# Stick-breaking attention on one core: sums of later key blocks with low parts on GpSimd, the last pair in a new order, and a weight panel's high part on GpSimd

## What is computed

```python
z = einsum('bqhd,bkhd->bhqk', q, k) * HD_B ** -0.5 + bias
u = where(mask, log_sigmoid(-z), 0.0)                # mask: key strictly before query
rev_excl = cumsum(u, axis=3, reverse=True) - u       # sum over later keys
A = where(mask, exp(log_sigmoid(z) + rev_excl), 0.0)
out = einsum('bhqk,bkhd->bqhd', A, v)
h = h + out @ w_out_b                                # output projection
```

## Time and profile before

| | us |
|---|---|
| median of 3 runs (1500.52 to 1502.69) | 1500.58 |
| the profiled execution | 1502.18 |
| its span, first to last instruction | 1500.4 |
| TensorE busy | 1476.8 |
| VectorE busy | 1181.6 |
| ScalarE busy | 827.7 |
| GpSimd busy | 333.6 |

### The profile page before, as it was taken

The page is one execution under the profiler, slowest core; times in us unless marked ns, Lnnn a source line. Parts: engine busy times, 40 slices in busy tenths (PEclk is TensorE's granted clock), DMA queues, the critical chain, the costliest instruction groups (busy, mean ns, idle before and its releaser), DMA issues.

```text
span 1500.4 us, 33609 instructions
## 1 busy us (share of the span) xinstructions
PE 1476.8 (98%) x12928; PEld 1397.7 (93%) x12928; DVE 1181.6 (79%) x2014; ACT 827.7 (55%) x1312; POOL 333.6 (22%) x330
## 2 busy tenths in 40 slices
PE   8999999999999999999999999999999999999998
PEld 8999999989999999999998888887699999999998
DVE  7866666667898988989834888888789989898753
ACT  6554444435664645546533777777756546364543
POOL 3000000002332232232142122112233332232221
PEclk9999999999999999999999999999999999999999
DMA  6233333223777877777425555543338777778621
GB/s 191 58 87 88 87 87 87 87 87 87 139 170 157 179 164 161 176 153 155 135 85 176 186 191 197 184 156 114 100 86 168 177 159 168 166 157 187 142 85 64
DMA packets 237716, 205.83 MB, mean 137 GB/s; under 512 B 8268, under 2 KB 224404, under 8 KB 237588
## 3 DMA queue, kind: packets, MB, share of 16 engines
q1 hardware_dynamic: 151346, 147.34, 31.6%
q0 software_dynamic: 68160, 47.20, 20.4%
q10 hardware_dynamic: 18082, 9.48, 2.3%
HBM read 192.19 MB, written 11.80 MB: 136 GB/s over the span
## 4 chain that ended last, share of the span: by engine, by line
PE 94%; DVE 2%; ACT 2%; issue 1%; DMA 0%; DVEq 0%; ACTq 0%
PE acc L2904 23%; PE acc L3227 18%; PE pL L3227 12%; PE pM L3227 9%; PE acc L3327 6%; PE pO L3227 3%; PE acc L3165 2%; PE pL L3025 1%; PE pL L3368 1%; PE pO L3401 1%; PE pM L3382 1%; PE acc L3444 1%; PE acc L3461 1%; PE pM L3094 1%; PE pM L3388 1%
## 5 line engine op out<-in xcount | busy, mean ns | idle before, releaser
L658 POOL TENSOR_TENSOR wlo<-wraw,whi 128x512 fp32r<-128x512 f32 x40 | 56.2, 1435 | 449.3 <-ACT whi L795 449.3
L2904 PE MATMUL acc<-xa_hi,whi 128*128 128x288 f32 x544 | 125.0, 311 | 0.2 <-DVE hT L2355 0.2
L881 ACT ACTIVATE hi<-wraw 128x1024 fp32r<-128x1024 f32 x60 | 63.7, 1061 | 104.2 <-DVE wraw L2025 104.2
L864 ACT ACTIVATE hi<-wraw 128x1024 fp32r<-128x1024 f32 x60 | 63.7, 1061 | 103.0 <-PE acc L3227 102.8
L2904 PE MATMUL acc<-xa_hi,wlo 128*128 128x288 f32 x544 | 116.5, 296 | 0.0
L2904 PE MATMUL acc<-xa_lo,whi 128*128 128x288 f32 x544 | 116.1, 295 | 0.0
L3227 PE MATMUL acc<-X_lo,hi 128*128 128x288 f32 x384 | 113.3, 295 | 0.0
L3227 PE MATMUL acc<-X_hi,lo 128*128 128x288 f32 x384 | 113.3, 295 | 0.0
L3227 PE MATMUL acc<-X_hi,hi 128*128 128x288 f32 x384 | 113.1, 294 | 0.0
L2040 DVE TENSOR_TENSOR lo<-wraw,hi 128x1024 fp32r<-128x1024 f32 x60 | 73.3, 1222 | 42.4 <-ACT hi L864 42.4
L3227 PE MATMUL acc<-H_hi,hi 128*128 128x288 f32 x336 | 99.3, 296 | 1.3 <-DVE lo L2046 1.3
(11 more groups left out here) (549 smaller groups left out, 5135.2 us busy)
## 6 DMA issues: line engine op xcount, KB each, us to landing
wraw<-in_w_up_dram SPq DMA_DIRECT2D x64, 512.0 KB, 6.4
wraw<-in_w_down_dram SPq DMA_DIRECT2D x64, 512.0 KB, 5.5
Kp<-in_cache_k_dram SPq DMA_DIRECT2D x32, 512.0 KB, 4.4
Vp<-in_cache_v_dram SPq DMA_DIRECT2D x32, 512.0 KB, 5.4
wraw<-in_w_in_a_dram SPq DMA_DIRECT2D x30, 512.0 KB, 5.6
wraw<-in_w_up_dram POOLq DMA_DIRECT2D x32, 256.0 KB, 4.8
S_even<-in_w_up_dram POOLq DMA_DIRECT2D x32, 256.0 KB, 6.3
S_odd<-in_w_up_dram POOLq DMA_DIRECT2D x32, 256.0 KB, 6.9
```

The lines of the kernel that those rows point to most:

```text
L658: ins = pool.tensor_tensor(wlo[s][:, k:k + 2, :], wraw[s][:, k:k + 2, :], whi[s][:, k:k + 2, :].bitcast(F32), ALU.subtract)
L864: act.activation(blocks4(hi02), by_rows(G % 2)[:, 0], ACT.Copy).then_inc(piece_hi, 1)
L881: act.activation(blocks4(hi31), by_depth(G % 2)[:, 0], ACT.Copy).then_inc(piece_hi, 1)
L2904: last = pe.matmul(acc[a][:, hf, 0:HALF], w[s][:, k, a * P:(a + 1) * P], x[k][:, hf * HALF:(hf + 1) * HALF], start=(k == 0 and n == 0), st ...
```

## The change

1. The sum of block 1 and the sum of blocks 3 and 2 is made once more ahead of use: `later_sum_0` on GpSimd (256 columns), `later_high_0` on ScalarE, `later_low_0` on GpSimd. It replaces block 1's last 256 columns in `uh` and `ul`, so that groups 4 and 5 need one pair of ones products instead of two.
2. `later_low_1` moves from VectorE to GpSimd. Counts of `u_lo`, `u_hi` and `bias_ready` change with it.
3. GpSimd's low part of the key and value weights is issued in two halves (`kv_low_half`) with sums between them.
4. The last pair has a new order on TensorE, VectorE and ScalarE.
5. The high part of output panel 1 is made by `high_panel` on GpSimd, four copies, ahead of the last pair's sums; ScalarE's `wsplit` there is gone.

The diff, cut in the order lists, which stand below as built:

```diff
@@ -173,10 +173,11 @@
         LATER = [slice(0, 128), slice(128, 384), slice(384, 768)]
-        S1_COLS, N_U = slice(256, 384), 8
-        H_AT, S1_HI = (1, 2, 3, 4, 7, 8), (5, 6)
-        LATER_AT = (1, 2, 4, 6, 7, 8)
-        U_AT = (1, 2, 4, 5, 7, 8)
+        S1_COLS, S0_COLS = slice(256, 384), slice(512, 768)
+        HIGH_AT = [{"u": (1, 2, 3, 4, 7, 9), "s1": (5, 6), "s0": (8, 10)},
+                   {"u": (1, 2, 3, 5, 7, 10), "s1": (4, 6), "s0": (8, 9)}]
+        POOL_AT = [{"a1": (1, 2), "l1": (3, 6), "a0": (5, 7), "l0": (8, 9)},
+                   {"a1": (1, 2), "l1": (3, 5), "a0": (4, 6), "l0": (7, 8)}]
         qT_at = (limit - NB * T * 4) // 64 * 64
@@ -445,6 +446,17 @@
+        def last_turn(j):
+            return isinstance(j, int) and j == NPAIR - 1
+        def high_count(j, what, n):
+            return 10 * j + HIGH_AT[last_turn(j)][what][n]
+        def pool_count(j, what, hh):
+            return 9 * j + 1 + POOL_AT[last_turn(j)][what][hh]
@@ -751,14 +763,58 @@
-                pool.wait_ge(u_lo, N_U * j + U_AT[hh])
+                pool.wait_ge(u_lo, 6 * j + hh + 1)
                 pool.tensor_tensor(tl[hh][:, S1_COLS], tl[hh][:, S1_COLS], tl[hh][:, 0:P], ALU.add).then_inc(bias_ready, 1)
+            def later_low_1(j, hh):
+                pool.wait_ge(u_hi, high_count(j, "s1", hh))
+                pool.tensor_tensor(ul[hh][:, S1_COLS], tl[hh][:, S1_COLS], uh[hh][:, S1_COLS].bitcast(F32), ALU.subtract
+                                   ).then_inc(bias_ready, 1)
+            def later_sum_0(j, hh):
+                pool.wait_ge(u_lo, 6 * j + hh + 3)
+                pool.wait_ge(bias_ready, pool_count(j, "a1", hh))
+                pool.tensor_tensor(tl[2 + hh][:, P:3 * P], tl[2 + hh][:, P:3 * P], tl[hh][:, P:3 * P], ALU.add
+                                   ).then_inc(bias_ready, 1)
+            def later_low_0(j, hh):
+                pool.wait_ge(u_hi, high_count(j, "s0", hh))
+                pool.tensor_tensor(ul[hh][:, S0_COLS], tl[2 + hh][:, P:3 * P], uh[hh][:, S0_COLS].bitcast(F32), ALU.subtract
+                                   ).then_inc(bias_ready, 1)
+            def kv_low_half(j, a, q):
+                cols = slice(a * P, (a + 1) * P)
+                if q == 0:
+                    pool.wait_ge(kv_hi, 2 * j + a + 1)
+                ins = pool.tensor_tensor(wlo0[:, 4 * q:4 * q + 4, cols], wraw0[:, 4 * q:4 * q + 4, cols],
+                                         whi0[:, 4 * q:4 * q + 4, cols].bitcast(F32), ALU.subtract)
+                if q:
+                    ins.then_inc(kv_lo, 1)
...
                 later_sum_1(j, 0)
-                kv_low(j + 2, 0)
+                kv_low_half(j + 2, 0, 0)
                 later_sum_1(j, 1)
+                later_low_1(j, 0)
+                kv_low_half(j + 2, 0, 1)
                 masked_bias(j + 1)
+                later_sum_0(j, 0)
+                later_low_1(j, 1)
+                later_sum_0(j, 1)
+                later_low_0(j, 0)
+                later_low_0(j, 1)
+            def high_panel(s, Pn, n_use):
+                pool.wait_ge(raw_landed[s], 32 * n_use)
+                pool.wait_ge(hi_done, Pn - 1)
+                for k in range(0, 8, 2):
+                    ins = pool.tensor_copy(whi[s][:, k:k + 2, :], wraw[s][:, k:k + 2, :])
+                ins.then_inc(hi_done, 1)
@@ -772,8 +828,15 @@
             split_low_unit(1).then_inc(lo_done, 1)
+            high_panel(1, U_OB // 2 + 1, U_OB // 4 + 1)
             later_sum_1(NPAIR - 1, 0)
             later_sum_1(NPAIR - 1, 1)
+            later_low_1(NPAIR - 1, 0)
+            later_sum_0(NPAIR - 1, 0)
+            later_low_1(NPAIR - 1, 1)
+            later_sum_0(NPAIR - 1, 1)
+            later_low_0(NPAIR - 1, 0)
+            later_low_0(NPAIR - 1, 1)
             pool.wait_ge(lo_done, U_OB // 2 + 1)
@@ -1433,9 +1496,15 @@
-                act.wait_ge(bias_ready, 3 * j + 2 + hh)
+                act.wait_ge(bias_ready, pool_count(j, "a1", hh))
                 act.wait_ge(R_full, 7 * j + hh + 2)
...
+            def later_high_0(j, hh):
+                act.wait_ge(bias_ready, pool_count(j, "a0", hh))
+                act.wait_ge(R_full, 7 * j + hh + 4)
+                act.activation(uh[hh][:, S0_COLS], tl[2 + hh][:, P:3 * P], ACT.Copy).then_inc(u_hi, 1)
@@ -1475,10 +1544,12 @@
                 u_high(j, 4)
+                later_high_0(j, 0)
                 weights(j, 0)
...
                 u_high(j, 5)
+                later_high_0(j, 1)
                 k_high(j + 1)
@@ -1499,22 +1570,23 @@
                 softplus(j, 3)
+                u_high(j, 2)
+                later_high_1(j, 0)
                 softplus(j, 4)
-                u_high(j, 2)
                 u_high(j, 3)
-                later_high_1(j, 0)
+                later_high_1(j, 1)
+                u_high(j, 4)
+                later_high_0(j, 0)
                 softplus(j, 5)
-                later_high_1(j, 1)
+                later_high_0(j, 1)
+                ob_high(NB - 2)
                 weights(j, 0)
-                u_high(j, 4)
+                u_high(j, 5)
                 new_factor(j)
                 new_weights(j)
-                u_high(j, 5)
                 weights(j, 1)
-                ob_high(NB - 2)
                 weights(j, 2)
                 weights(j, 3)
-                wsplit(1, U_OB // 2 + 1, U_OB // 4 + 1)
                 weights(j, 4)
@@ -1541,6 +1613,7 @@
             act.wait_ge(kv_stored, 64 * NPAIR)
+            act.wait_ge(hi_done, U_OB // 2 + 1)
             enter_mlp(1, U_OB, n_norm["mlp1"], GMLP1)
@@ -2583,7 +2656,7 @@
                 if g == 0:
-                    dve.wait_ge(bias_ready, 1 if isinstance(j, int) and j == 0 else 3 * j - -1)
+                    dve.wait_ge(bias_ready, 1 if isinstance(j, int) and j == 0 else 9 * j - 4)
                 nd = len(GROUPS[g])
@@ -2603,15 +2676,9 @@
                 cols = slice(GCOL[g], GCOL[g] + GW[g])
-                dve.wait_ge(u_hi, N_U * j + H_AT[n])
+                dve.wait_ge(u_hi, high_count(j, "u", n))
                 dve.wait_ge(sp_done, 6 * j + n + 1)
                 dve.tensor_tensor(ul[hh][:, cols], tl[n][:, 0:GW[g]], uh[hh][:, cols].bitcast(F32), ALU.subtract
-                                  ).then_inc(u_lo, 1)
-            def later_low_1(j, hh):
-                dve.wait_ge(u_hi, N_U * j + S1_HI[hh])
-                dve.tensor_tensor(ul[hh][:, S1_COLS], tl[hh][:, S1_COLS], uh[hh][:, S1_COLS].bitcast(F32), ALU.subtract
                                   ).then_inc(u_lo, 1)
@@ -2711,14 +2778,12 @@
                 logits_in(j, 5)
-                later_low_1(j, 0)
                 t_copy(j + 1, 7)
...
                 sp_add(j, 4)
-                later_low_1(j, 1)
                 minus_later(j, 2)
...
@@ -3376,12 +3439,13 @@
                     pe.wait_ge(n_dve, 6 * j + 1)
-                pe.wait_ge(u_lo, N_U * j + U_AT[n])
+                pe.wait_ge(u_lo, 6 * j + n + 1)
                 tri = slice(GCOL[g], GCOL[g] + GW[g])
...
                     pe.matmul(pM[:, 0:GW[g]], tri_r[:], u[:, tri], start=u is uh[hh], stop=False)
-                pe.wait_ge(u_lo, N_U * j + LATER_AT[n])
-                later = [(LATER[g], GW[g])] if g < 2 else [(LATER[2], GW[2]), (LATER[1], GW[2])]
+                if g:
+                    pe.wait_ge(bias_ready, pool_count(j, ("l1", "l0")[g - 1], hh))
+                later = [(LATER[g], GW[g])]
                 for cols, end in later:
@@ -3555,20 +3619,20 @@
                 ob_prompt_part(1, 2)
-                ob_prompt_part(0, 3)
                 later_sums(j, 0)
                 new_sums(j)
+                ob_prompt_part(0, 3)
                 later_sums(j, 1)
...
                 later_sums(j, 3)
+                ob_prompt_part(0, 5)
+                later_sums(j, 4)
+                ob_prompt_part(1, 5)
+                later_sums(j, 5)
                 new_values(j)
-                later_sums(j, 4)
-                ob_prompt_part(0, 5)
-                later_sums(j, 5)
-                ob_prompt_part(1, 5)
                 ob_prompt_part(0, 6)
...
                 weighted(j)
```

More of the change, by code:

```diff
@@ L2753, in last_pair @@
                 new_sp(j)
-                ob_low(3)
-                sp_add(j, 0)
                 logits_in(j, 2)
                 logits_in(j, 3)
+                sp_add(j, 0)
+                past_store(j)
                 sp_add(j, 1)
-                attn_out(j - 1)
-                past_store(j)
+                u_low(j, 0)
                 logits_in(j, 4)
-                u_low(j, 0)
+                ob_low(3)
+                sp_add(j, 2)
+                minus_later(j, 0)
                 u_low(j, 1)
                 logits_in(j, 5)
-                minus_later(j, 0)
-                sp_add(j, 2)
+                ob_low(4)
+                u_low(j, 2)
+                minus_later(j, 1)
                 sp_add(j, 3)
-                ob_low(4)
-                later_low_1(j, 0)
-                minus_later(j, 1)
```

(17 more changed lines are left out.)

## The result

| us | before | after |
|---|---|---|
| median of the runs | 1500.88 (6 runs) | 1510.3 (6 runs, 1508.67 to 1511.99) |
| the profiled execution, its span | 1502.18, 1500.4 | 1510.45, 1508.7 |
| first matmul of `weighted` to the next, a steady pair | 33.32 | 34.08 |
| the same, last pair | 27.09 | 31.16 |
| from the last `weighted` to the end of the span | 424.4 | 424.6 |

The ratio of the times is 1.0061 (95% interval 1.0048 to 1.0074). The kernel is slower by 9 us, where 1509.0 was forecast against 1500.58. In the two profiled spans the difference is 8.3 us: 4.0 up to the last pair's start, 4.1 in the last pair, 0.2 behind it. The 4.0 understate the steady pairs.

What follows compares the result with a forecast made beforehand. TensorE, busy 98% of the span, was taken as the bound. Steady pairs +4.6 us and last pair +4.0 us on the 1502.18 us profiled execution made 1510.8, forecast as a median of 1509.0; range 1498 to 1514.

Steps and rivals of the forecast that it cites:

- the likeliest case: Whole kernel: port turns lengthen the steady pairs and the last pair; 1504 to 1514 us, given 62%.
- the last sum: Closing arithmetic: 1510.8 us for the profiled execution, lowered to the runs' median, which stood 1.6 us below: 1509.0.
- Edit 2: Seven steady pairs: new GpSimd work makes VectorE wait at the SBUF port; +0.65 us a pair, both savings counted, +4.6 us.
- Edit 1: Steady pairs: sums five and six lose two 256-column matmuls each; 0.46 us a pair, 3.2 us if nothing else moves.
- the bound: Steady pairs without any port wait: past_AT and minus_later(5) hold the end, 0.39 of 0.46 us a pair remain, -2.7 us.
- Edit 3: Last pair: the new order gains nothing and port turns delay `weighted` to near 1080; +4.0 us, bounds -3.3 and +6.
- sp_add(5), ob_low(6) and u_low(5) each wait for most of one of them: Last pair: these VectorE operations wait behind GpSimd's panel 1 low-part pieces, as the longest L1727 did (+1.09 us).
- `weighted` starts at 1075.85 against 1076.04: nothing gained: Last pair's new order laid out without port waits: matmul and wait savings are offset by the chain behind sum six.
- Where both queue, they alternate.: SBUF port: queued VectorE and GpSimd operations take turns; L1727 took 1.84 us beside L658 instead of 0.75.
- Edit 4: GpSimd's four copies for panel 1's high part, 0.60 us each near 1054.5, cost next to nothing; at 1.29, 2 us more.
- TensorE's waits for the new low parts themselves cost nothing: Steady pairs: later_low_1(0) is done near 1001.6 for use at 1004.7, later_low_0(0) near 1008.9 for 1010.8.
- The rival of the waits for sums: Steady pairs: GpSimd loses every turn, TensorE waits before the ones product; 1.5 to 2 us a pair, 1513 to 1518, 5%.

Runs made afterwards that it cites:

- experiment 2: Changed kernel, but in the seven pairs before the last the six new GpSimd operations work on 4 columns: pitch 33.06 us, total 1502.84 us (1.0011).
- experiment 3: Changed kernel, steady pairs only: later_low_0 gated on u_low(4) and u_low(5), later_high_1(1) and later_low_1(1) moved earlier; 1504.48 us (1.0017).
- experiment 5: Steady pairs as in experiment 3, last pair as before the change, two fill matmuls moved ahead of the second cached-key logits: 1500.55 us (0.9994).
- experiment 8: Changed kernel with GpSimd's low part of panel 1 held until VectorE's product pastO is done: last pair 30.28 us, total 1509.08 us (1.0051).
- experiment 6: Changed kernel, but in the last pair alone the six new GpSimd operations work on 4 columns: last pair 28.43 us, total 1508.46 us (1.0045).
- experiment 11: Changed kernel with six extra 512-column matmuls filling TensorE's wait before output slice 5 in the last pair: last pair 29.65 us, total 1508.91 us (1.0045).
- experiment 9: Changed kernel with the last pair's minus_later(5) ahead of new_out and pastO on VectorE: last pair 28.03 us, total 1508.92 us (1.0053).
- experiment 10: Changed kernel, last pair: minus_later(3) before ob_low(5), slice 5's first matmuls behind the fifth sum, minus_later(5) before new_out and pastO; 1509.71 us (1.0054).
- experiment 7: Changed kernel without GpSimd's high_panel; ScalarE makes panel 1's high part in the last pair again: last pair 30.77 us, total 1509.02 us (1.0047).

## Why the prediction was right, and where it was right by chance

The total (1509.0 against 1510.3) and the direction held; the likeliest case came true. A slip of 0.2 us is in the last sum: 1510.8 less 1.6 is 1509.2.

- **Edit 2, port turns in the steady pairs.** The mechanism and the place were right: four VectorE operations longer by 0.28, 0.09, 0.55 and 0.35 us, together 1.27, where the steps said 0.28, 0.08, 0.54 and 0.44, together 1.34. The group of the difference has a mean of 1.12 us (1.1 was said), a 256-column operation takes 0.74 (0.73), TensorE waits 0.78 a pair before the transposes (0.9). The pitch grew by 0.76 us instead of 0.65, which over seven pairs is 5.3 us instead of 4.6. Experiments 2 and 3 show it from both sides.
- **Edit 1, fewer matmuls.** Without port turns 0.26 us a pair were left (33.32 to 33.06, experiment 2), not the 0.39 of the bound. The step had named what holds the end, `past_AT`: TensorE waits 0.16 us for it in experiment 2, behind VectorE's copy. It was mis-sized, not missed. Experiment 5 adds that filling TensorE's other idle time, 0.31 us behind ScalarE's copy of the keys, gives nothing in the gated pairs, since VectorE and ScalarE hand over as late as before.
- **Edit 3, the last pair.** +4.07 us against the +4.0 of the sum, and the working behind it was mostly wrong. "sp_add(5), ob_low(6) and u_low(5) each wait for most of one of them" failed: 0, 0 and 0.28 us in the changed kernel's profile (u_low(5) lost 0.28 to 1.05 us where experiments left its surroundings alone, see experiment 8). "`weighted` starts at 1075.85 against 1076.04: nothing gained" failed too: with the small operations on 4 columns and the clock at 1.00 the last pair is still 1.3 us longer than the old one (28.43 against 27.09, experiment 6), of which 0.55 at u_low(5) and 0.31 at `pastO` are turns with panel 1's low part. What stands in its place: the small operations cost 1.2 us (28.43 instead of 29.65, experiments 6 and 11), the chain of `new_out`, `pastO` and the last subtraction behind sum six 1.6 (28.03 instead of 29.65, experiments 9 and 11; 0.3 of it is `pastO`'s turn with panel 1's low part, and 1.0 would come back anyway), and the lower clock 1.5 (31.16 instead of 29.65). With the old 27.09 these make 31.4, 0.2 too much: the first two were each measured with the other in place and the clock at 1.00, and that all three add is not shown. The step names the first two, the small operations without a price of their own and the chain as 2.5 us with 1.4 us of matmuls beside it; the clock is in no step. That the three sum to the 4.0 of the forecast is luck. The low part of panel 1 did start where it was said (1075.23), but two of its four pieces, not all, ran over 1.7 us (2.45 and 1.72), and the first by its own waiting.
- **"Where both queue, they alternate."** They do so in some runs (ob_low(6) +1.09 in experiment 10, exactly the figure used) and not in others (the changed kernel, where two VectorE operations went first). As a price it is the most that these runs show one operation to lose, not a value.
- **Edit 4.** Right: 0.61 us a copy (0.60 was said), at 1058.3 to 1060.6 (1054.5 and the 4 us by which the pair starts later), and no cost to TensorE (experiment 7).
- **"TensorE's waits for the new low parts themselves cost nothing".** Right in the steady pairs. The rival of the waits for sums never showed.

## What to carry to other kernels

In these runs work moved to GpSimd was free only where VectorE read PSUM or waited. Gate each such operation on the step that precedes one, as experiment 3 did: the same work then cost 0.14 us a pair (33.20 against 33.06) instead of 1.02. Before trading matmuls for helper work, read how late the other engines' chain hands over: of the 0.46 us of matmuls saved a pair 0.26 came out as a shorter pair even without turns, though TensorE was busy 98% of the time. And a long idle time of TensorE can be dearer than its length, as the clock may fall at its end.

## What the runs showed of the hardware

- The granted TensorE clock fell to half (0.50 in the window from 1075 to 1080 us) for 6.8 us in the changed kernel's profile and for 3.4 us in those of experiments 2, 3, 7, 8 and 10, each time within 1 us of the end of a wait; in the 5 us up to that end TensorE had been busy 2.2 to 2.4 us. 512-column matmuls then followed one another every 0.43 us instead of 0.23. The same stretch with 2.40 us did not bring it down in experiment 9, and no profile with the wait filled or shortened (experiments 11 and 6) shows a fall. It cost 1.5 to 1.8 us in the changed kernel's profiled execution.
- A GpSimd operation that waits for the port can be passed by VectorE operations that follow each other closely: 2.45 us for a 1.29 us subtraction, with two of them ahead, though its recorded start was 0.03 us before the first of them.
